# One encoder layer with 32 experts on one core: second expert matrix fetched eight neighbouring rows to a partition, activations turned by every eighth column

## What is computed

```python
def expert_block(args):
    xb, e = args
    gu = xb @ w_gu[e] + b_gu[e]
    g = jnp.minimum(gu[:, :D_EXPERT], SWIGLU_LIMIT)
    lin = jnp.clip(gu[:, D_EXPERT:], -SWIGLU_LIMIT, SWIGLU_LIMIT)
    act = g * jax.nn.sigmoid(SWIGLU_ALPHA * g) * (lin + 1.0)
    return act @ w_down[e] + b_down[e]
```

## Time and profile before

| | us |
|---|---|
| median of 3 runs | 1678.56 |
| lowest and highest | 1677.52, 1680.78 |
| the profiled execution, whole time | 1681.96 |
| its span, first to last instruction | 1680.1 |

### The profile page before, as it was taken

How to read it: one execution, slowest core, us unless ns; L and a number is a source line. 1 busy time by engine, 2 the same in 40 slices (tenths; PEclk the granted TensorE clock), 3 DMA queues, 4 the chain that set the end, 5 groups by cost and what they waited for, 6 DMA issues and landing times.

```text
span 1680.1 us, 21768 instructions
## 1 busy us (share of the span) xinstructions
PE 1603.1 (95%) x7657; PEld 1180.8 (70%) x7657; DVE 1290.3 (77%) x1004; ACT 1099.7 (65%) x1036; POOL 353.7 (21%) x265
## 2 busy tenths in 40 slices
PE   5999899999986999999999999999999999999993
PEld 4877688888864777777777777777777777777772
DVE  6646643424687899988899988899888899898881
ACT  4446662233355787777787777787777777777762
POOL 6400000000034222332222332222332222332210
PEclk7999999999997999999999999999999999999997
DMA  7320001414766999999999999999999999999963
GB/s 253 128 75 20 1 1 64 138 63 147 301 245 237 355 381 371 371 363 373 374 375 382 367 364 370 381 374 377 367 368 369 380 374 375 368 367 369 375 252 119
DMA packets 101765, 476.00 MB, mean 283 GB/s; under 512 B 11016, under 2 KB 11552, under 8 KB 68832
## 3 DMA queue, kind: packets, MB, share of 16 engines
q1 hardware_dynamic: 93504, 448.18, 69.5%
q0 software_dynamic: 7888, 27.23, 7.1%
q10 hardware_dynamic: 336, 0.08, 0.0%
HBM read 456.69 MB, written 19.66 MB: 284 GB/s over the span
## 4 chain that ended last, share of the span: by engine, by line
PE 93%; DMA 3%; ACT 2%; DVE 2%; issue 1%; SPq 0%; POOL 0%; ACTq 0%; POOLq 0%; DVEq 0%
PE ps L1642 28%; PE ps L1663 14%; PE ps L1645 14%; PE ps L1668 7%; PE ps L1380 6%; PE ps L1382 6%; PE ps L1381 6%; PE ps L1407 4%; PE ps L1501 2%; PE ps L1634 2%; PE ps L1475 2%; DMA xg<-h_rows,slot_rows 1%; PE ps L1654 1%; DMA x_sb<-in_x 1%; PE ps L1466 1%
## 5 line engine op out<-in xcount | busy, mean ns | idle before, releaser
L1169 DVE TENSOR_TENSOR l_w<-a_w,h_w 128x2048 fp32r<-128x2048 f32 x384 | 869.5, 2292 | 37.4 <-ACT h_w L793 35.9
L793 ACT ACTIVATE h_w<-a_w 128x2048 fp32r<-128x2048 f32 x384 | 731.8, 1916 | 249.1 <-PE ps L1645 172.2
L1642 PE MATMUL ps<-h_w,xt_hi 128*96 128x512 f32 x1024 | 286.7, 401 | 1.3 <-DVE xt_lo L1305 1.3
L1642 PE MATMUL ps<-h_w,xt_lo 128*96 128x512 f32 x1024 | 278.8, 394 | 0.0
L1645 PE MATMUL ps<-l_w,xt_hi 128*96 128x512 f32 x1024 | 278.7, 394 | 0.0
L943 POOL TENSOR_TENSOR mark_sb<-ones 1x1 f32<-1x1 f32 x96 | 93.8, 977 | 840.2 <-ACT y_sb L842 832.4
L1642 PEld LDWEIGHTS ps<-h_w,xt_lo 128*96 128x96 f32 x1024 | 166.1, 162 | 71.0
L1645 PEld LDWEIGHTS ps<-l_w,xt_hi 128*96 128x96 f32 x1024 | 166.1, 162 | 71.0
L1642 PEld LDWEIGHTS ps<-h_w,xt_hi 128*96 128x96 f32 x1024 | 163.6, 162 | 69.5 <-DVE xt_lo L1305 1.5
L1663 PE MATMUL ps<-h_w,at_hi 128*96 128x512 f32 x512 | 169.2, 412 | 0.0
L1663 PE MATMUL ps<-h_w,at_lo 128*96 128x512 f32 x512 | 160.4, 394 | 0.0
(11 more groups left out here) (227 smaller groups left out, 1718.2 us busy)
## 6 DMA issues: line engine op xcount, KB each, us to landing
a_w<-in_w_gate_up SPq DMA_DIRECT2D x256, 1024.0 KB, 7.8
a_w<-in_w_down SPq DMA_DIRECT2D x128, 1024.0 KB, 6.1
w_raw<-in_w_in SPq DMA_DIRECT2D x8, 2048.0 KB, 9.1
w_raw<-in_w_out SPq DMA_DIRECT2D x2, 2048.0 KB, 8.6
x_sb<-in_x SPq DMA_DIRECT2D x4, 512.0 KB, 6.2
w_raw<-in_w_in SPq DMA_DIRECT2D x2, 1024.0 KB, 17.4
w_raw<-in_w_mem_kv SPq DMA_DIRECT2D x1, 2048.0 KB, 13.9
x<-in_x SPq DMA_DIRECT2D x4, 512.0 KB, 5.1
```

The source lines that it names most:

```text
L793: nc.scalar.activation(h_w[m % H_SLOTS][:], a_w[m % A_SLOTS][:], ACT.Copy).then_inc(wh_done, 1)
L1169: nc.vector.tensor_tensor(l_w[m % A_SLOTS][:], a_w[m % A_SLOTS][:], h_w[m % H_SLOTS][:].bitcast(F32), ALU.subtract).then_inc(wl_done, 1)
L1642: nc.tensor.matmul(ps[0:SLOTS, n, :], x_part[:, k, :], w_h[:, n * COLS:(n + 1) * COLS], start=False, stop=False)
```

## The change

The down matrix is seen as `"e (p k) n -> e p k n"`: partition p holds rows 8p to 8p+7, and part q carries rows 8p+2q and 8p+2q+1, which are neighbours in memory. What a partition gets in a part is thus one run of 8 KB where it was two of 4 KB that lay 512 KB apart; from one partition to the next the source moves on by 32 KB where it moved by 4 KB. The size of a part, the buffers, the waits and the order stay. To match, the stationary operand for chunk k has to hold activation 8p+k on partition p, so `turn_act` no longer turns 128 neighbouring columns but every eighth column, 32 bytes apart.

```diff
-        wdn = w_down[0].rearrange("e (k p) n -> e p k n", p=P)
+        wdn = w_down[0].rearrange("e (p k) n -> e p k n", p=P)
...
+            act_by_row = act_sb[:].rearrange("s (p k) -> s k p", k=KD)
+
             def turn_act(j):
                 pe.wait_ge(act_ready, j + 1)
                 for k in range(KD):
-                    last = turn(6 + k // 4, (k % 4) * SLOTS, act_sb[:, k * P:(k + 1) * P])
+                    last = turn(6 + k // 4, (k % 4) * SLOTS, act_by_row[:, k, :])
                 last.then_inc(at_ps, 1)
```

## The result

| | before | changed |
|---|---|---|
| median, first comparison (5 runs each) | 1679.06 us | 1688.81 us, ratio 1.0057 (1.0044 to 1.0070) |
| median, second comparison (27 and 8 runs) | 1680.29 us | 1687.42 us, ratio 1.0039 (1.0026 to 1.0053) |
| profiled execution, whole time and span | 1681.96, 1680.1 us | 1688.48, 1686.6 us |

The change makes the kernel slower, by 0.4 to 0.6%. The forecast was 30.7 us more; measured were 9.7 and then 7.1. The sign was right, the size three to more than four times too large. The first median, 1688.81 us, lies inside the stated range (1683 to 1714), near the end that the range took from rival B.

The account below looks back on a forecast made before the run. TensorE was taken to bound the loop. Down loads counted 0; seven strided turning loads a job, 137 ns extra each, 0.96 us x 32 jobs = 30.7 us, gave 1678.56 + 30.7 = 1709.3 us, range 1683 to 1714.

Parts of the forecast that it names:

- rival B: Turning's weight loads: a jump halves their rate to 0.84 to 0.88 ns a column, 5.6 to 6.9 us more, 1684.8; chance 0.20.
- The bound: Loop over the experts: TensorE's own instructions set the 35.91 us a job; transfers have some 5 us of each to spare.
- The loads: Down loads in 8 KB runs: gain 0 in the loop, between -1 and +1 us outside; 32 KB source pitch harmless.
- the gather: Second gather of token rows, before the loop, 22.5 us to land: faster down loads bring it forward 0.9 us at most.
- One sign: Down loads in the profile after: they should land no later than before, when they landed 6.1 us after issue.
- How a turning is paced: Eight turnings in a row: the identity's 82 ns sets the pace until the weight load, now about 60 ns, is longer.
- The first load of eight: First turning's weight load in each job: hidden under the product ahead, so only the other seven set the pace.
- The price of a column: Turning's strided weight load: 1.71 ns a column from VectorE's sums, 219 ns a load, 30.7 us in all.

## Why the prediction was right in kind and wrong in size

- **The bound.** Right. The loop is TensorE's own time: 0.20 us more on it in each job are 0.20 us more between jobs, and in the loop ScalarE's copies waited for nothing but TensorE, 1.0 us at the longest.
- **The loads.** Right: no cost and no gain (1.0002), half the packets for the down matrix, the gather 22.46 against 22.50 us, and the pitch of 32 KB harmless, and even one of 64 KB on the gate-up weights. The row on HBM row pitch in the Trainium skill ("DMA: Bandwidth & Descriptors") lists nothing under 512 KB, where it has 207 GB/s against 214 for its full rate, so it could only suggest this; the runs show it. One sign was off by a little: the down loads land 0.1 us later, not earlier or alike.
- **How a turning is paced.** Right, and shown by setting the turnings apart: the longer of identity (82 ns) and weight load. The first load of eight is hidden, as said. That in a row a second is hidden too and the product behind the last pays in its place was not foreseen; that the count stays at seven even so is luck.
- **The price of a column: the step that failed.** The term of the sum that was mis-sized is the time that a strided weight load takes for a column. The prediction read "I take 1.71 ns for a column", carried over from VectorE's sums, hence 219 ns a load and 137 ns for each of seven turnings. The steady pace is 111 ns, 0.87 ns a column if the load fills it, so 29 ns for each of seven: 0.20 us a job, 6.4 us in all in place of 30.7. The load's own record shows 206 ns where the prediction looked for about 300, eight matmuls 1.02 us where it looked for 1.78. The rate is half of the 1.71 and, within the reading, that of TensorE's ordinary loads (0.84 to 0.88 ns). That was rival B, which said 36.1 us between jobs and 5.6 to 6.9 us in sum. Its number came true; its reason isn't shown. The other jumps have a pace of 0.120 to 0.123 us, 0.94 to 0.96 ns a column, which is twice the prediction's 0.47 for neighbouring columns rather than the ordinary rate.
- **Where I should have looked closer.** VectorE pays for reading with a stride of 32 bytes 0.98 ns a number, more than the 0.67 I read off its small sums, so the price from VectorE was real, for VectorE. What didn't follow was that the memory sets it for every reader. The row on the very port in question, an ordinary weight load of 128 columns at 190 ns, was at hand and had been given the smaller chance. Of its load duration B was 16 ns short (190 against a median of 206).
- **The median.** The first comparison's 9.7 us is 3 more than the loop explains; a second effect of the turning or of the loads isn't seen in the second comparison or with each part alone. The profiled executions scatter by as much outside the loop; that this made the 3 us is likely, but the executions behind that median left no trace of the parts.

## What to carry to other kernels

Before a data layout is changed to please the DMA, look at whether the loop waits for DMA at all: here it had, by the prediction's estimate, 5 us of each 36 to spare, and fewer, larger packets bought nothing. When a stationary operand has to be read with a stride, expect its weight load to set the pace in a row of short matmuls, and put those between long products, where it cost 0.02 us for eight here, or let an engine with time to spare write the operand in order, which left the loop as it was before. Take the price of an access pattern from the port that will pay it, however few rows there are for it, and not from another engine.

## What the runs showed of the hardware that was not expected

- A turning weight load of 128 float32 columns slows from 140 to 212 ns with the smallest jump, 8 bytes, to 218 at 28 bytes, and is at 202 with 32 bytes (means over 256 loads). The page "SBUF — State Buffer" of the Trainium skill (on cachelines) lets one expect that two hits on a line of 16 bytes are enough for full speed; the load with 8 bytes between columns contradicts it.
- The same stride of 32 bytes costs VectorE 0.98 ns for each number read (2225 against 1222 ns for 1024), TensorE's load about 0.5 for each column in its duration (206 against 140 ns for 128) and 0.23 in the pace of a row of turnings (111 against 82 ns). Writing in jumps of 512 bytes costs VectorE 0.79 ns a number (2027 against 1220).
- Weights whose source moves on by 32 KB (down) or 64 KB (gate-up) from one partition's 8 KB to the next one's were fetched at 366 GB/s from 560 to 1640 us, with TensorE busy for all of it.
